# Last rows of layer 0 placed by the tensor engine, other rows read back earlier, a 128-row gather and layer-norm sums in four column tiles

## What is computed

```python
for i in range(2):
    mix = rg_lru_block(x, ...) if i == 0 else pool_mixer(x, ...)
    x = layer_norm(ALPHA * x + mix, ln_g[i, 0], ln_b[i, 0])
    ffn = hier_moe(x, ...)
    x = layer_norm(ALPHA * x + ffn, ln_g[i, 1], ln_b[i, 1])

def layer_norm(x, g, b):
    mu = mean(x); var = mean((x - mu) ** 2)
    return (x - mu) * rsqrt(var + 1e-5) * g + b

def hier_moe(x, ...):        # 4 groups of 4 experts, 512 wide
    gsel = argmax(x @ wg + bg)                       # one group for each row
    topv, topi = top_k(expert logits of that group, 2)
    wt = softmax(topv) * softmax(x @ wg + bg)[gsel]
    out = sum over the two experts of wt * (silu(x @ Wgate) * (x @ Wup)) @ Wdown
```

## Time and profile before

| What | Value |
|---|---|
| Median of 3 runs | 1574.06 us (1572.89 to 1574.29) |
| The profiled execution | 1576.47 us |
| Its span from first to last instruction | 1574.7 us |
| TensorE busy | 1444.7 us, 92% of the span |
| VectorE busy | 490.9 us, 31% |
| ScalarE busy | 373.2 us, 24% |
| DMA traffic | 488.02 MB, mean 310 GB/s |
| Chain that ended last | TensorE 69%, DMA 22%, VectorE 5% |
| Mean granted TensorE clock | 0.954 of full speed |

### The profile page before, as it was taken

The page is one execution under the profiler, slowest core; times in us unless marked ns, Lnnn a source line. Parts: engine busy times, 40 slices in busy tenths (PEclk is TensorE's granted clock), DMA queues, the critical chain, the costliest instruction groups (busy, mean ns, idle before and its releaser), DMA issues.

```text
span 1574.7 us, 20389 instructions
## 1 busy us (share of the span) xinstructions
PE 1444.7 (92%) x8908; PEld 794.3 (50%) x8908; DVE 490.9 (31%) x1028; ACT 373.2 (24%) x556; POOL 22.4 (1%) x34
## 2 busy tenths in 40 slices
PE   6999998999899998998999858979999999889995
PEld 6999998996643432332343225745333233224321
DVE  4867768554330020020020016542103003001202
ACT  4565566333401021021021011240101102001100
POOL 0000000000000000000000000000000000000000
PEclk8999999999799999999999977988999999999998
DMA  9554554642289999999999981436999999999992
GB/s 299 191 173 136 174 174 146 229 161 107 82 331 402 427 418 397 427 427 398 427 428 396 427 332 60 160 120 282 391 427 418 396 427 427 391 428 427 409 411 111
DMA packets 89061, 488.02 MB, mean 310 GB/s; under 512 B 5325, under 2 KB 59277, under 8 KB 61357
## 3 DMA queue, kind: packets, MB, share of 16 engines
q1 hardware_dynamic: 83984, 463.75, 74.0%
q0 software_dynamic: 2464, 13.37, 2.8%
q10 hardware_dynamic: 2522, 9.59, 1.8%
HBM read 476.15 MB, written 14.47 MB: 312 GB/s over the span
## 4 chain that ended last, share of the span: by engine, by line
PE 69%; DMA 22%; DVE 5%; issue 2%; ACT 1%; DVEq 0%; POOL 0%; SPq 0%; ACTq 0%; POOLq 0%
DMA ring<-in_moe_w_down 19%; PE ps L1060 18%; PE ps L1043 17%; PE ps L972 5%; PE ps L866 4%; PE ps L868 4%; PE ps L867 4%; PE ps L1107 2%; PE ps L898 2%; PE ps L900 2%; PE ps L899 2%; PE ps L880 2%; PE ps L997 1%; DMA ring<-in_lru_w_in 1%; PE ps L906 1%
## 5 line engine op out<-in xcount | busy, mean ns | idle before, releaser
L1043 PE MATMUL ps<-ring,xsel 128*64 128x512 f32 x2048 | 472.8, 613 | 30.0 <-DMA ring<-in_moe_w_gate_up 30.0
L1060 PE MATMUL ps<-ring,work 128*32 128x512 f32 x3072 | 346.2, 595 | 12.2 <-DMA ring<-in_moe_w_down 12.2
L1043 PEld LDWEIGHTS ps<-ring,xsel 128*64 128x64 f32 x2048 | 143.7, 141 | 330.6 <-issue 278.7
L1060 PEld LDWEIGHTS ps<-ring,work 128*32 128x32 f32 x3072 | 91.8, 109 | 223.7 <-issue 205.4
L1581 DVE SCALAR_TENSOR_TENSOR arena<-arena,ps 64x512 f32<-64x512 f32 x32 | 21.7, 679 | 567.9 <-ACT work L750 567.9
L866 PE MATMUL ps<-operands,whi 128*128 128x288 f32 x512 | 154.4, 302 | 2.4 <-DVE ring_lo L1184 2.4
L868 PE MATMUL ps<-operands,ring_lo 128*128 128x288 f32 x512 | 152.4, 298 | 0.0
L867 PE MATMUL ps<-ring_lo,whi 128*128 128x288 f32 x512 | 151.6, 296 | 0.0
L1184 DVE TENSOR_TENSOR ring_lo<-ring,whi 128x1024 fp32r<-128x1024 f32 x96 | 115.8, 1222 | 72.8 <-ACT whi L582 72.5
L582 ACT ACTIVATE whi<-ring 128x1024 fp32r<-128x1024 f32 x96 | 100.8, 1058 | 147.4 <-PE ps L868 89.9
L749 ACT ACTIVATE arena<-ps 64x512 f32<-64x512 f32 x32 | 18.9, 590 | 411.0 <-PE ps L1043 411.0
(11 more groups left out here) (293 smaller groups left out, 1192.2 us busy)
## 6 DMA issues: line engine op xcount, KB each, us to landing
ring<-in_moe_w_gate_up SPq DMA_DIRECT2D x128, 2048.0 KB, 19.6
ring<-in_moe_w_down SPq DMA_DIRECT2D x64, 2048.0 KB, 22.3
ring<-in_lru_w_in SPq DMA_DIRECT2D x16, 2048.0 KB, 9.4
ring<-in_lru_w_out SPq DMA_DIRECT2D x8, 2048.0 KB, 9.4
x_rows<-xtok ACTq DMA_DIRECT2D x4, 1024.0 KB, 4.1
ring<-in_pool_w SPq DMA_DIRECT2D x4, 1024.0 KB, 19.3
xtok<-in_x_prompt SPq DMA_DIRECT2D x2, 1024.0 KB, 9.0
ring<-in_lru_w_a SPq DMA_DIRECT2D x8, 256.0 KB, 5.3
```

The costliest lines, as they stand in the source:

```text
L1043: last = mm(ps[half * ES:(half + 1) * ES, e % 2, :], xsel[:, k, e * ES:(e + 1) * ES], wt[:, half * 512:(half + 1) * 512], start=(k == 0), ...
L1060: last = mm(ps[rows:rows + QB, 2 + r, :], act[:, e % 2, f * W + slots0:f * W + slots0 + QB], wt[:, d * 512:(d + 1) * 512], start=start, st ...
```

## The change

1. **End of layer 0.** The last window's rows no longer go to DRAM and back. The put of that window is gone in layer 0. A new matrix `place` (128 by 288) holds, for each slot of the last window, a 1 in the column of its token, and for partitions 96 to 127 a 1 in columns 256 to 287. SP's queue, after its last weight chunk of layer 0 has landed, reads back the rows of the other windows: 128 rows to `xtok[:, 0]`, 128 to `xtok[:, 2]`, and the last 32 under ZS in `xtok[96:128, 1]`. TensorE adds, for each block of 128 features, two products of the read rows with the identity and two products of the tile with ZS and `place` in PSUM. Five of the 16 blocks have their identity products before the wait for `z_done`, three behind it. ACT and DVE each normalise half of ZS. The ten idle products are gone.
2. **Zeros.** So that rows that were not put hold zeros, ACT's queue fills `n_rows` with zeros from `place` in head 1 (1 KB pieces).
3. **Gather.** `fetch` brings 128 rows, not 96; rows 96 to 127 are tokens 96 to 127, which nobody uses.
4. **Sums of norms 0 and 2.** `sum_blocks` takes four blocks at once: four products with a 128x32 matrix `share`, one in each 32-column part of TensorE's array, for z in bank 7 and four for the squares in bank 6. `total` adds the four parts: DVE and ACT copy the banks to SBUF, and two products with `ones` give mean and mean square everywhere. For norm 0 two of the four rounds run inside the output projection, the squares are made there too, and `zsum` with its adds is gone.

```diff
@@ SP, end of layer 0's loads
+                    n = base + PER_WIN - 1
+                    eng.wait_ge(ring_ready[slot_of(n)], eng.snap(n_win * 64 + (ready_at(n) - 64)))
+                    eng.wait_ge(rows_in[0], eng.snap(n_win * 16 + 16))
+                    eng.wait_ge(back_in, 48)
+                    for dst, (t0, m) in zip((xtok[:, 0, :], xtok[:, 2, :], xtok[W:128, 1, :]), TILES):
+                        eng.dma_start(dst, n_rows[t0:t0 + m, :]).then_inc(back_in, 16)
@@ POOL
-                    eng.indirect_dma_start(XS, None, x_rows[l], bass.IndirectOffsetOnAxis(src_now[0:W, 0:1], 0))\
+                    eng.indirect_dma_start(xtok[:, 0, :], None, x_rows[l], bass.IndirectOffsetOnAxis(src_now[:, 0:1], 0))\
                        .then_inc(rows_in[l], 16)
-                put()
+                if l == 1:
+                    put()
@@ ACT
+                if h == 1:
+                    for t0, m in TILES:
+                        eng.dma_start(n_rows[t0:t0 + m, :].rearrange("t (a c) -> t a c", c=256),
+                                      place[0:m, 0:256].unsqueeze(1).to_broadcast([m, D // 256, 256])).then_inc(back_in, 16)
+            for p in range(NPART, PARTS_OUT):
+                high_part(PARTS_LRU + p)
+                c = p // PARTS_CHUNK - 2
+                if p % PARTS_CHUNK == 1 and c >= 0:
+                    squares(0, range(2 * c, 2 * c + 2))
-                    eng.wait_ge(rows_out[0], eng.snap(n_win * 16))
-                    eng.wait_ge(rows_in[0], eng.snap(n_win * 16 + 16))
-                    for i, (t0, m) in enumerate(TILES):
-                        eng.dma_start(xtok[0:m, i, :], n_rows[t0:t0 + m, :]).then_inc(back_in, 16)
+                    eng.wait_ge(znorm_ready[0], n_win)
+                    for q in range(2):
+                        c = slice(q * 512, (q + 1) * 512)
+                        eng.activation(ZS[:, c], ZS[:, c], ACT.Identity, scale=zr[0:W, :], bias=zn[0:W, :])\
+                           .then_inc(rows_last[0], 1)
@@ TensorE
+            def sum_blocks(n, r):
+                for bank, ready, src in ((7, z_ready[n], [z[:, 4 * r + j, :] for j in range(4)]),
+                                         (6, sq_ready[n], sq_of[n][4 * r:4 * r + 4])):
+                    eng.wait_ge(ready, 4 * r + 4)
+                    for j in range(4):
+                        last = mm(ps[32 * j:32 * (j + 1), bank, 0:T], share[:, :], src[j], start=(r == 0),
+                                  stop=(r == KD // 4 - 1), tile_position=(0, 32 * j))
+            def total(n):
+                eng.wait_ge(sums_copied, n + 2)
+                mm(ps[:, 7, 0:T], ones[:, :], mean[:, :], start=True, stop=True)
+                mm(ps[:, 6, 0:T], ones[:, :], nmr[:, :], start=True, stop=True).then_inc(stat_done[n], 1)
@@ in the output projection
+                if i in (5, 7):
+                    sum_blocks(0, (i - 5) // 2)
@@ end of layer 0
-                    eng.wait_ge(rows_out[0], eng.snap(n_win * 16))
-                    stay_awake(10)
-                    eng.wait_ge(back_in, 48)
+                    eng.wait_ge(back_in, 96)
+                    for k in range(5):
+                        rows_back(k)
                     eng.wait_ge(z_done[0], eng.snap(n_win * 4 + 4))
+                    for k in range(5, 8):
+                        rows_back(k)
                     for k in range(KD):
                         if k >= 8:
                             eng.wait_ge(x_ready[1] if k % 2 == 0 else x_odd, k // 2 - 3)
-                        for i, (t0, m) in enumerate(TILES):
-                            last = nc.tensor.transpose(ps[:, k % 8, t0:t0 + m], xtok[0:m, i, k * 128:(k + 1) * 128],
-                                                       ident[0:m, 0:m])
-                        last.then_inc(back_turned, 1)
+                            rows_back(k)
+                        if k in (0, 4):
+                            eng.wait_ge(rows_last[0], k // 4 + 1)
+                        elif k in (8, 12):
+                            eng.wait_ge(z_done[0], eng.snap(n_win * 4 + (k // 4 + 3)))
+                        zk, bank = xtok[:, 1, k * 128:(k + 1) * 128], BACK_BANK[k % 8]
+                        mm(ps[:, bank, 0:TP], zk, place[:, 0:TP], start=False, stop=False)
+                        mm(ps[:, bank, TP:T], zk, place[:, TP:T], start=False, stop=True).then_inc(back_turned, 1)
@@ DVE
-                    if k == 0:
-                        link(V.tensor_copy(zsum[:, :], z[:, 0, :]))
-                    elif k < KD - 1:
-                        link(TT_(zsum[:, :], zsum[:, :], z[:, k, :], ALU.add))
@@ last window of layer 0
+                    eng.wait_ge(znorm_ready[0], n_win)
+                    for q in range(2, 4):
+                        c = slice(q * 512, (q + 1) * 512)
+                        TS_(ZS[:, c], ZS[:, c], zr[0:W, :], zn[0:W, :], ALU.mult, ALU.add).then_inc(z_done[0], 1)
...
```

More of the change, by code:

```diff
@@ L161, in encoder_step @@
         ones = sb("ones", [128, 128])
-        onesd = sb("onesd", [128, 128])
+        place = sb("place", [128, T])
+        share = sb("share", [128, 32])
         before = sb("before", [128, 128])
@@ L259, in encoder_step @@
         TL = carve(sqm, 0, 2, TG)
+        sq_last = [sqm[:, 0:T], sqm[:, T:2 * T], uext[:, 0, 0:T], uext[:, 1, 0:T]]
+        sq_of = {0: [arena[:, i * T:(i + 1) * T] for i in range(KD - 4)] + sq_last, 2: sq_last * (KD // 4)}
         xtf = xtok[:, :, :].rearrange("p i d -> p (i d)")
@@ L292, in encoder_step @@
         sq_ready = {i: sem(f"sq_ready{i}") for i in (0, 2)}
-        sq_used = {i: sem(f"sq_used{i}") for i in (0, 2)}
-        zsum_ready = {i: sem(f"zsum_ready{i}") for i in (0,)}
+        sq_used = sem("sq_used")
+        sums_copied = sem("sums_copied")
         stat_done = {i: sem(f"stat_done{i}") for i in (0, 2)}
@@ L470, in _ @@
             eng.memset(ones[:, :], 1.0).then_inc(consts, 1)
-            eng.memset(onesd[:, :], 1.0 / D).then_inc(consts, 1)
+            eng.memset(share[:, :], 1.0 / (32 * D)).then_inc(consts, 1)
             eng.wait_ge(consts, 4)
@@ L651, in _ @@
             high_of_y(3)
-            for p in range(PARTS_LRU + NPART, PARTS_LRU + PARTS_OUT):
-                high_part(p)
             def squares(n, blocks):
@@ L658, in squares @@
                     eng.wait_ge(z_ready[n], k + 1)
-                    if k >= 2:
-                        eng.wait_ge(sq_used[n], k - 1)
-                    eng.activation(sq[:, k % 2, :], z[:, k, :], ACT.Square).then_inc(sq_ready[n], 1)
+                    if n == 2 and k >= 4:
+                        eng.wait_ge(sq_used, k // 4)
+                    eng.activation(sq_of[n][k], z[:, k, :], ACT.Square).then_inc(sq_ready[n], 1)
+            for p in range(NPART, PARTS_OUT):
[3 more added lines that the diff above has]
+                    squares(0, range(2 * c, 2 * c + 2))
             def layer_norm(n, vec):
-                squares(n, range(12 if n == 2 else 0, KD))
+                squares(n, range(12, KD))
+                eng.wait_ge(stat_done[n], 1)
+                eng.activation(nmr[:, :], ps[:, 6, 0:T], ACT.Copy).then_inc(sums_copied, 1)
                 eng.wait_ge(var_ready[n], 1)
@@ L901, in _ @@
                     last.then_inc(parts_used, 1)
[L903 to L921, removed]
             def stay_awake(n):
                 for _ in range(n):
-                    mm(ps[:, 2, 0:T], onesd[:, :], prmT[:, 0:T], start=True, stop=True)
+                    mm(ps[:, 2, 0:T], ones[:, :], prmT[:, 0:T], start=True, stop=True)
             def moe(l):
@@ L1110, in _ @@
                 if g >= 1:
-                    pool_stats(g - 1)
-            pool_stats(NG - 1)
-            mm(ps[0:1, 0, 0:2], onesd[:, 0:1], onesd[:, 0:2], start=True, stop=True).then_inc(stat_done[2], 1)
+                    sum_blocks(2, g - 1)
+            sum_blocks(2, NG - 1)
+            total(2)
             moe(1)
@@ L1148, in _ @@
             V.memset(uext[:, :, :], 0.0)
+            V.memset(place[:, :], 0.0)
             V.memset(valid[:, 0:2, :], 1.0)
@@ L1313, in ln_stats @@
                 eng.wait_ge(stat_done[n], 1)
+                V.tensor_copy(mean[:, :], ps[:, 7, 0:T]).then_inc(sums_copied, 1)
+                eng.wait_ge(stat_done[n], 2)
                 link(V.tensor_copy(mean[:, :], ps[:, 7, 0:T]))
@@ L1620, in moe @@
                 eng.wait_ge(kept[l], eng.snap(n_win + 1))
-                put_to(n_win)
+                if l == 0:
+                    eng.wait_ge(back_in, 48)
+                    V.tensor_copy(place[W:128, TP:T], ident[W:128, W:128])
+                    for t0, m in TILES:
+                        TS_(place[0:W, t0:t0 + m], iota_f[0:W, 0:m], float(t0), slot_f[0:W, 0, bass.ds(n_win - 1, 1)],
+                            ALU.add, ALU.is_equal)
+                else:
+                    put_to(n_win)
                 for b in range(4):
```

25 lines of the change are left out of this document (15 added, 10 removed).

## The result

The changed kernel takes 1528.11 us (median of 4 runs, 1526.69 to 1531.12), the kernel before 1573.47 (4 runs, 1572.42 to 1574.29): ratio 0.9715, 95% interval 0.9698 to 0.9731. The profiled execution took 1528.34 us with a span of 1526.6 us, 48.1 less than the span before.

| stretch | before, us | after, us | difference | forecast |
|---|---|---|---|---|
| start to second copy of norm 0's mean | 381.73 | 373.97 | -7.8 | -5.5 |
| to the first window product of layer 0 | 51.3 | 48.1 | -3.2 | about 0 |
| windows of layer 0 | 487.0 | 480.2 | -6.8 | about +0.4 |
| end of layer 0, to the mixer's first DVE step | 37.2 | 21.6 | -15.7 | -14.0 |
| pooling mixer and norm 2, to the mean | 57.0 | 52.5 | -4.5 | -6.3 |

What follows compares the result with a forecast made beforehand. TensorE was taken to bound the output projection, the DMA weight stream the expert windows, a weight-free chain of waits the gap between layers. 14.0 + 5.5 + 6.3 - 1.0 = 24.8 us gained: 1549 us median, range 1545 to 1553.

Steps and rivals of the forecast that it cites:

- Gather and zeros: Ten gathers of 128 rows instead of 96, and zeros written in head 1: 1 us lost in all.
- the wide gather is quicker: Rival on the gathers: 128 rows cost less time than 96, giving 1546 us; chance 0.10.
- End of layer 0: Last window's product to pooling mixer: rows placed by TensorE without the DRAM round trip, gain 14.0 us.
- The 2.2 us for a recovery of the clock: While rows are placed at layer 0's end: 4.4 us at half speed, losing 2.2 us.
- The first rival: End of layer 0: the clock stays low while rows are placed, price 8.1 us, giving 1557; chance 0.13.
- 951.3 us for the mixer's start at the low clock: After layer 0's placing: pooling mixer starts at 941.0 at full clock, 951.3 at low; gain 16.2 or 5.9 us.
- the read-back is late: Rival at layer 0's end: SP's read lands at 926 or later, delaying the products 4 us, 1553; chance 0.10.
- Norm 0: Layer 0's first norm: mean copy 7.5 us earlier, less 2.0 us of products in the projection; gain 5.5 us.
- The 2.0 us of added products in the projection: Output projection, where TensorE is full: two rounds of 8 tile products, 2 x 0.98 us, paid against the norm's gain.
- Pooling mixer and norm 2: Between the layers: shorter sums free product groups 2 and 3, 3.0 us, and the norm's end, 3.3: gain 6.3 us.
- the slower rival: Low clock carries into the pooling mixer as TensorE waits for DVE; four groups add 29 us, 1578; chance 0.03.
- if the windows' length moves by more than 4 us: Expert windows of both layers: lengths expected as before within 2 us; a move over 4 us marks the prediction wrong.

## Why the prediction was wrong

- **The step that failed** is "Gather and zeros". It priced the wide gather by its own pieces, 0.49 or 0.34 us each, and took +1.0 us, with -2 us as the best case ("*the wide gather is quicker:* 1546"). The gather alone measures -20.4 us. Both prices of the piece were near enough (0.50 and 0.31 us in the stream). Missing was a second payer: while a 96-row gather is in the queues, the weight pieces on the same engines take 0.98 instead of 0.62 us. Eight gathers lie within a stream that bounds the kernel, so each dip is paid in full: the windows are 16.4 us shorter by the wide gather alone and 16.9 in the changed kernel, 2.1 us a dip. The other 4 us of the 20.4 are not shown to come from the gather; in its trace 3.7 us lie at the end of layer 0, in the transposes' clock.
- The error is one of reading. "The windows' own gathers run beside weights where nothing shows the price" was untrue: the 257 GB/s at a share of 1.00 stand in the trace of before, around 601 us. I read the table of stretches for shares only, saw 0.95, and took a full share for a full rate. The earlier trace rows gives 389 GB/s over layer 1's windows, where the undisturbed stream makes 421 to 434.
- Why the width matters is open: 112 rows are as bad as 96 (274 to 326 and 285 to 343 GB/s in the kernel before) while 128 leave the stream at 421 GB/s or more, and no run here shows the cause. Had I asked what a gather does to the *other* packets on the engines, this would have been a rival.
- **End of layer 0**, -14.0: -15.7 in the traces, -12.6 alone. From the last product to the first placed block 6.4 us were forecast, 6.6 measured; for the blocks 13.9 and 14.2; for the read-back 8.9 and 8.7. The 2.2 us for a recovery of the clock were not paid: TensorE idled 1.3 and 1.1 us, not 2, and the clock stayed at 1.00. The first rival is out in this kernel. Its 951.3 us for the mixer's start at the low clock, 10.3 us after 941.0, is a term that no run shows: the placing took 14.2 us at 1.00 here, and its mean clock was 1.00 in four of the five other kernels with it and 0.96 in the fifth (the end of layer 0 alone). The second, "the read-back is late", came in the kernel with this part alone, though not in the way it names: the read was slow, its start was not late.
- **Norm 0**, -5.5: -7.8. The mean's chain was right (3.7 forecast, 4.0 measured). The 2.0 us of added products in the projection hardly show: its last product ends at 369.9, against 370.4 before, and at 368.5 to 369.2 in the four other traces without them, 368.9 to 370.3 in the five others with them. So this profile of before was itself over 1 us long here, and against the other four the step is -5.8 to -6.3. Why the products cost so little is open.
- **Pooling mixer and norm 2**, -6.3: -4.5. The end, 4.6 forecast, took 5.3 us, and two groups ran half at the low clock (1.6 and 1.7 us). This is the start of the slower rival, whose condition, shorter waits becoming idle time, held at two of four groups. It was far from its price of 29 us: the clock rose again within each group, to 1.00 by 932 and by 966. That price takes four groups at the low clock from end to end, which no run shows; the longest group in the traces took 11.08 us (gather of 112 rows). With the sums alone that second fall did not occur at all, so after 1.76 us of idle time the clock was sometimes down (0.55, 9.69 us) and sometimes not (1.00, 8.00 us).
- The two norms together measure 11.6 us alone, 11.8 forecast. Against the table's rows this is luck in part, one miss offsetting the other.
- My own sign that the prediction fails, "if the windows' length moves by more than 4 us", is the one that did.

## What to carry to other kernels

Where DMAs bound a stretch, read GB/s beside the share, in windows of some 5 us around each small transfer: a dip at full share that comes with the transfer (here 257 GB/s at 1.00) can be a tax on its neighbours (here 0.98 us a weight piece instead of 0.62). Try a gather into all 128 partitions even when 96 are used, if the tile has the room: it took 20.4 us off here by itself, and 112 took off nothing. This was measured for rows of 8 KB beside a stream that bounds the kernel. Price a change in a shared resource by what it does to the other users of it, not by its own pieces alone.

## What of the hardware was not expected

- A gather of 8 KB rows into 96 or 112 partitions takes the weight stream from some 430 to between 274 and 343 GB/s for about 10 us, with the engines busy throughout (shares of 0.99 to 1.02); one into 128 leaves it at 421 to 434. The first costs 0.50 us a piece and the second 0.31, and a 16 KB weight piece beside them 0.98 and 0.62.
- Moving 492.23 MB instead of 488.02 took less time.
- The put of a window's rows, which *reads* 96 partitions of SBUF, hardly disturbs the stream: over the 10 us from the issue of each of the three puts within layer 0's windows it moved 402, 427 and 426 GB/s before, 418, 429 and 427 after.
- The clock stayed at 1.00 through 8.8 us of nothing but transposes in one kernel, and was down to 0.60 and then 0.50 after some 2 us of the same transposes in the kernel before.
- Seven short products in TensorE's 3.85 us ahead of the mixer kept its clock up (8.02 us instead of 9.57 for the first group, with 1.20 us of idle time ahead of it).
